# Moving the output projection's parts ahead of the value products in TensorE's slot

## The reference

```python
o = concatenate([diff_attn(...), dsa_attn(...)], axis=-1)
m = o @ w_out
x = x + ga1 * rms_norm(m, g_post_mix)
```

## Time and profile before

| | |
|---|---|
| time, median of 3 runs | 1704.54 us (1704.43 to 1708.21) |
| the profiled execution's own time | 1709.16 us |
| its span, first to last instruction | 1707.4 us |
| its mean granted TensorE clock | 0.964 of full speed |
| PE / PEld / DVE / ACT / POOL busy | 91% / 76% / 44% / 32% / 23% of the span |

### The profile page before, as it was taken

How to read it: one execution, slowest core, us unless ns; L and a number is a source line. 1 busy time by engine, 2 the same in 40 slices (tenths; PEclk the granted TensorE clock), 3 DMA queues, 4 the chain that set the end, 5 groups by cost and what they waited for, 6 DMA issues and landing times.

```text
span 1707.4 us, 23915 instructions
## 1 busy us (share of the span) xinstructions
PE 1561.9 (91%) x8999; PEld 1297.4 (76%) x9019; DVE 749.9 (44%) x1751; ACT 547.8 (32%) x1134; POOL 393.7 (23%) x335
## 2 busy tenths in 40 slices
PE   5699999995788989998769999999999999999996
PEld 2486899994344555555439999999999999999995
DVE  0603799996856665565460312213022130311305
ACT  1735322212355565565362111122111211212112
POOL 0511111110011111011146221323223132231325
PEclk9999999996699999999779999999999999999998
DMA  8310357615333444242251201102111011110006
GB/s 273 99 44 26 107 170 225 188 65 184 102 102 114 129 116 142 88 127 57 69 175 57 67 26 49 49 25 59 40 49 49 25 49 49 49 43 30 0 1 123
DMA packets 148567, 146.94 MB, mean 86 GB/s; under 512 B 12125, under 2 KB 129182, under 8 KB 148490
## 3 DMA queue, kind: packets, MB, share of 16 engines
q1 hardware_dynamic: 147258, 141.46, 28.0%
q0 software_dynamic: 1232, 4.46, 1.4%
HBM read 126.60 MB, written 19.29 MB: 85 GB/s over the span
## 4 chain that ended last, share of the span: by engine, by line
PE 84%; DVE 5%; issue 3%; ACT 3%; DMA 2%; POOL 2%; SPq 1%; POOLq 0%; DVEq 0%; ACTq 0%
PE S L1951 31%; PE PJ L1707 15%; PE T L1966 11%; PE PJ L1870 7%; PE PJ L1966 5%; PE S L1809 4%; PE T L1787 2%; PE PJ L1911 2%; PE PJ L1914 2%; DMA ada_more<-in_w_ada 1%; DVE sc L1511 1%; PE S L1656 1%; PE S L1726 1%; DVE scrap L1338 1%; ACT aT L1120 1%
## 5 line engine op out<-in xcount | busy, mean ns | idle before, releaser
L1951 PE MATMUL S<-h2h,gh 128*128 128x352 f32 (+1 forms) x1056 | 346.6, 328 | 2.0 <-DVE top L1594 2.0
L1951 PE MATMUL S<-h2h,gl 128*128 128x352 f32 (+1 forms) x1056 | 345.9, 328 | 0.0
L1951 PE MATMUL S<-h2l,gh 128*128 128x352 f32 (+1 forms) x1056 | 345.6, 327 | 0.0
L1619 DVE TENSOR_TENSOR hv<-sg,S 128x352 f32<-128x352 f32 (+1 forms) x66 | 35.1, 532 | 496.5 <-ACT sg L1250 496.5
L1951 PEld LDWEIGHTS S<-h2h,gh 128*128 128x128 f32 x1056 | 198.8, 188 | 2.6 <-issue 2.2
L1951 PEld LDWEIGHTS S<-h2l,gh 128*128 128x128 f32 x1056 | 199.5, 189 | 0.4
L1951 PEld LDWEIGHTS S<-h2h,gl 128*128 128x128 f32 x1056 | 198.5, 188 | 0.0
L1338 DVE TENSOR_SCALAR_CACHE_REDUCE scrap<-work,cand 128x384 uint8<-128x384 f32 (+6 forms) x217 | 180.1, 884 | 1.1
L1707 PE MATMUL PJ<-hTh,wh 128*128 128x352 f32 (+3 forms) x504 | 168.9, 335 | 0.0
L1707 PE MATMUL PJ<-hTh,wl 128*128 128x352 f32 (+3 forms) x504 | 166.0, 329 | 0.0
L1707 PE MATMUL PJ<-hTl,wh 128*128 128x352 f32 (+3 forms) x504 | 166.0, 329 | 0.0
(11 more groups left out here) (207 smaller groups left out, 2406.3 us busy)
## 6 DMA issues: line engine op xcount, KB each, us to landing
graw<-in_w_gu SPq DMA_DIRECT2D x44, 512.0 KB, 4.9
ada<-in_w_ada SPq DMA_DIRECT2D x20, 1024.0 KB, 7.6
draw<-in_w_down SPq DMA_DIRECT2D x22, 512.0 KB, 3.3
wraw<-in_w_in SPq DMA_DIRECT2D x20, 512.0 KB, 5.5
q_scratch<-qst SPq DMA_DIRECT2D x8, 544.0 KB, 2.9
xin<-in_x_p SPq DMA_DIRECT2D x8, 512.0 KB, 3.5
ada_more<-in_w_ada SPq DMA_DIRECT2D x4, 1024.0 KB, 12.3
xt<-in_x_p SPq DMA_DIRECT2D x8, 512.0 KB, 4.8
```

The lines of the kernel that those rows point to most:

```text
L1951: last = pe.matmul(S[u % 2][:, 512 * part:512 * part + n], wp[:, slot, k, 128 * part:128 * part + 128], hp[:, k, c0:c0 + n], start=(k == 0 ...
```

## The change

In every slot that has one, the part of the output projection is issued before the value products and after the transposes; nothing else moves, and no instruction is added or removed. `out_projection` keeps its own waits (the weights, `m_out`, `rank_read`, the freed banks of the head outputs, `o_read`), and the products keep theirs. In slots without a part the order stays as it was.

```diff
@@ -1888,6 +1888,8 @@
                     pe.wait_ge(o_ready, diff_count(s))
                     bank = t_wait_free(pe, ("o", s))
                     pe.transpose(bank[:, 0:r], ob[0:r, s % 2, :], ident[0:r, 0:r]).then_inc(filled(("o", s)), 1)
+                if out_part(slot):
+                    out_projection(*out_part(slot))
                 if 2 <= slot < NSTEPS + 2:
 
                     s = slot - 2
@@ -1914,8 +1916,6 @@
                             last = pe.matmul(PJ[0][0:r, 0:128], aT[0:w, 0, j, 0:r],
                                              vsb[0:w, vt_, 128 * i:128 * i + 128], **edge)
                     last.then_inc(pv_done, 1)
-                if out_part(slot):
-                    out_projection(*out_part(slot))
                 for q in range(2):
                     t = tie_stage(slot, 2 + q)
                     if t and 512 * q < nkeys(t):
```

## The result

| | before | after |
|---|---|---|
| median of 5 runs each, us | 1706.32 (1704.43 to 1708.21) | 1714.17 (1713.48 to 1716.15) |
| the profiled execution's own time, us | 1709.16 | 1713.73 |
| its span, us | 1707.4 | 1712.0 |
| mean granted TensorE clock | 0.964 | 0.965 |

The medians differ by 7.9 us. The ratio is 1.0044 with an interval of 1.0031 to 1.0056, that is 5.3 to 9.6 us slower. The forecast was 3.0 us slower, 1707.5 us, with no measurable change as the likeliest case and a range up to 1711 us, so the range was missed on the slow side. The forecast started from the first three runs of before (1704.54 us); with five runs their median is 1.8 us higher, which explains that much of the distance and not more.

What follows compares the result with a forecast made beforehand. The prediction took TensorE, 84% of the chain that ended last, as the bound. A 5.9 us loss less gains of 1.7 and 1.2 us made +3.0 us on 1704.54 us, so 1707.5 us, range 1703.5 to 1711 us.

Steps and rivals of the forecast that it cites:

- no measurable change: Whole kernel: a difference within 5.1 us (0.3%), which a measurement cannot tell from no change; chance 0.77.
- head chain: Differential head's output: VectorE reads and squares products, GpSimd makes RMS factor, VectorE scales, TensorE transposes; covered by the 3.44 us part.
- the chain's price: From the products' modelled end to the next slot's head transpose: 2.01 us; waits in tiles 1, 2, 3, 8, 5.9 us lost.
- The waits of L1890: Head transpose waits for VectorE's `ob` in slots 4 to 6 of tiles 1, 2, 8, barely 3: 6.5 us become 11 to 12.5 us.
- The first rival: Handover from products to VectorE costs more and larger tiles pay too: 1710.4 us at 0.25 us, 1713.4 us at 0.5 us; chance 0.15.
- the gain of slot 6: The part covers the wait ahead of the products, about 1.2 us in the large tiles' slots 6, of 1.7 us gained.
- The net is 5.9 - 1.7 - 1.2 = +3.0 us: Whole kernel: head transpose loss, less the covered wait ahead of the products, less ScalarE's earlier start in slot 7.
- no stall: `out_projection`'s strictest wait, `m_out` in slot 5: at least 1.5 us lies between in tile 1, the copy takes 0.6 us.
- Other waits of the moved step: `out_projection`'s own waits, now ahead of the products: `m_out`, `o_read` and bank waits all met in time.
- 0.1 to 0.2 us behind it: Sign in the profile after: the part starts this long behind the head transpose in 32 slots.
- The gain of L1827 in slots 7: ScalarE starts its backlog earlier behind the last part, so TensorE waits less for probability copies: 1.2 us gained, ends 0 and 3.9 us.
- one more fall: TensorE's clock falls again after new idle times in tiles 1, 2 and 8: about 3.2 us, 1710.7 us; chance 0.05.

Runs made afterwards that it cites:

- run 1: Against the kernel before, only the parts of slots 3 to 5 moved ahead of the products; slot 6 kept the old order: ratio 1.0051, +8.7 us.
- run 2: Against the kernel before, only the part of slot 6 moved ahead of the products: ratio 0.9991, -1.5 us.
- run 3: Against the kernel before, parts moved only in tiles 4 to 7: ratio 0.9987, -2.2 us.
- run 4: Against the kernel before, parts moved only in tiles 1, 2, 3 and 8: ratio 1.0056, +9.6 us.
- experiment 5: Against the changed kernel, head transpose put behind the part, ahead of the products: 1698.45 us against 1708.05 us before, ratio 0.9944.
- run 7: Changed kernel, but VectorE scales the head by a factor it already has, not waiting for GpSimd's RMS factor: ratio 0.9983 to the kernel before, -2.9 us.
- run 13: Changed kernel, but five of a first part's waits issued at the end of the slot before, behind its products: 1712.90 us against 1708.50 us before.
- run 9: Changed kernel, but the five last waits of each first part issued four times over: 1730.47 us against 1708.79 us for the kernel before.
- run 11: Against the kernel before, head transpose put last, behind products and part: 1731.28 us, ratio 1.0129.
- run 10: Against the kernel before, head transpose put between the products and the part: 1705.82 against 1708.79 us, ratio 0.9979.
- run 8: The changed kernel again, unaltered: 1715.65 us against 1708.05 us for the kernel before, ratio 1.0043.
- run 14: The changed kernel once more, unaltered: 1714.96 us against 1708.50 us for the kernel before, ratio 1.004.
- run 6: Changed kernel, but a first part's semaphore waits issued ahead of the head transpose: ratio 1.0056 to the kernel before, +9.6 us.

## Why the prediction was right and wrong

**Right: what bounds these slots, and what the part covered.** The head chain was hidden under the part and no longer is. Runs 1 to 5 and 7 show it: the loss is in slots 3 to 5 of the short tiles, goes from the time when the chain is shortened, and turns into a gain when the part covers the chain again.

**Right: the chain's price and where it is paid.** The waits of L1890 were to become 11 to 12.5 us and are 11.2 us, 4.7 us more than before where the sum had 5.9 us. Slot by slot they are 1.29 us in (1, 4) for 1.2 forecast, 0.94 for 1.0 in (1, 6), 0.41 for 0.57 in (2, 4), 0.58 for 0.67 in (8, 4); in tile 3, where 0.3 us was forecast, none is new. The first rival, a dearer handover, is out: it is 0.04 us with 128 rows too, and no such wait appears in slots 4 and 5 of tiles 5 to 7.

**Right: the gain of slot 6.** The gap ahead of L1911 in slots (5, 6) and (7, 6) is gone: the products follow the part at once, as in slot (7, 6) after, where the part's 786.14 + 3.60 us is followed at 789.67. L1827 in (1, 7) waits 0.59 us for 0.7 forecast. Run 2 puts the slot at -1.5 us.

```profile
786.14 3.60 PE L1870 MATMUL PJ<-wout,oT 128*128 128x512 f32 x8
789.67 1.53 PE L1913 MATMUL PJ<-aT,vsb 128*64 128x128 f32 x24
```

**Wrong: the sum.** The step that failed is "The net is 5.9 - 1.7 - 1.2 = +3.0 us", and in it "no stall" for the part's own waits, put at nothing. The loss was 6.5 to 7.9 us by the medians of three sets of runs, because three costs are missing from the sum. As read from the traces they are 2.3, 1.3 and 1.5 us. With the chain's 1.2 us less this gives 3.0 + 2.3 + 1.3 + 1.5 - 1.2 = 6.9 us, an estimate, for the 7.1 to 7.9 us that the traces show behind the first moved part.

- *The part's own waits, under "Other waits of the moved step".* I asked only whether each was met ("no stall") and took met waits as free. Before, they stood behind the products, with 0.6 to 1.9 us of TensorE's work queued. After, they stand behind one transpose, often a late one. The sign "0.1 to 0.2 us behind it" in 32 slots came true in 20 (0.11 to 0.21 us): the other 12, all of them first parts, start 0.28 to 0.35 us behind. Run 13 puts the cost at 2.3 us in these slots. The four first parts in slots 5 of tiles 4 to 7 pay nothing; there the head transpose is not late, as in slot (4, 5) after:

```profile
598.34 0.28 PE L1890 MATMUL T<-ident,ob 128*128 128x128 f32 x1
598.45 3.60 PE L1870 MATMUL PJ<-wout,oT 128*128 128x512 f32 x8
```

Tile 3 and tiles 4 to 7 came out 1.6 us worse together than foreseen. Six of the twelve slots stand there, and run 13 got 1.3 us back in them. Run 9 shows the cost itself at 0.05 to 0.07 us per wait in the same twelve slots.
- *Where a stall goes.* The gain of L1827 in slots 7 was counted as final. VectorE, now later against TensorE, took it back: the first transpose of slot (2, 1) waits 1.12 us for 0.60 us before, and (3, 1) 0.79 for 0.45 us. Together with the slots around them this is the +0.52 and +0.74 us of the table. Runs 1 and 2 show whose cost this is: with slot 6 alone moved the two rows are +0.53 and +0.74 us, with slots 3 to 5 alone both are 0.00 us. So it is the give-back of slot 6's own gain, and not a cost of the head chain. The timeline of slot (2, 1) shows what stretched, first before, then after:

```profile
479.90 2.36 POOL L875 TENSOR_TENSOR msb<-msb,xt 128x1024 f32<-128x1024 f32 x1 [1.40 <-DVE msb L1444]
...
481.18 1.22 DVE L1528 TENSOR_SCALAR sc<-sc,rinv 128x256 f32<-128x256 f32 x1
...
482.46 0.44 PE L1787 MATMUL T<-ident,sc 128*128 128x128 f32 x2 [0.60 <-DVE sc L1528]
```

```profile
481.59 2.35 POOL L875 TENSOR_TENSOR msb<-msb,xt 128x1024 f32<-128x1024 f32 x1 [1.84 <-DVE msb L1444]
...
482.37 1.72 DVE L1528 TENSOR_SCALAR sc<-sc,rinv 128x256 f32<-128x256 f32 x1
...
484.14 0.44 PE L1787 MATMUL T<-ident,sc 128*128 128x128 f32 x2 [1.12 <-DVE sc L1528]
```

- *The clock.* I gave one more fall a chance of 0.05 and sought it in the tiles of the new waits. It fell right behind those of tile 1, near 485 us in slots (2, 1) and (2, 2), to its lower level (granted clock 0.50 from 488 to 491 us). The row of the table there is 1.48 us longer; the four products of L1809 took 1.65 us for 0.92 us. Every trace with the changed order in slots 3 to 5 of tile 1 shows a fall between 469 and 500 us, run 7 among them, which was not slower than before. So do runs 2 and 11, where these slots are not moved, and run 2 was not slower either; before, run 3, run 10 and both runs of the order of experiment 5 show none. So this is an added cost of about 1.5 us and not the main cause of the loss. What sets it off is not shown: run 2 has none of the new waits of the head transpose and the same +1.48 us, but its slot (2, 1) begins with a longer wait, 1.13 us for 0.60 us; run 1 has the new waits and not this one. The Trainium skill (TensorE: Matmul & The Clock Gate, Why this matters for your kernels) says that idle gaps of TensorE between bursts bring the low clock back. The trace of the kernel after agrees: the clock fell behind slots in which TensorE idled more than before. Run 2 does not bear it out: from 465 to 485 us its TensorE was busy for 15.99 us, as before, and the clock fell all the same.

```profile
482.44 0.44 PE L1787 MATMUL T<-ident,sc 128*128 128x128 f32 x2 [1.13 <-DVE sc L1528]
```

The row above is slot (2, 1) of run 2. How often the kernel before loses 3 us in slot (8, 3) can't be told from one profile: the traces of the changed kernel in runs 8 and 14 have no such fall there, nor has run 3, whose tile 8 is in the order of before.

**What carried the wrong probability.** Rival 1 had the right outcome with a wrong mechanism. That the missing terms have the same sign may be no accident: I had listed what each instruction waits for and not what is issued, or goes by, while it waits.

## What to carry to other kernels

A dense block whose result no engine needs soon can cover a long chain. Put it ahead of the instruction that waits for the chain, not ahead of the one that starts it; here the same move with the head transpose behind the part gave -10 us instead of +8 us. When a step moves, count its semaphore waits as work of the queue that it moves into: they were free where TensorE had work queued, and cost time where it had just run dry. Before an instruction moves later, look at who waits for its result in an engine that works in order (run 11).

## What the runs showed of the hardware

- A semaphore wait that has long been met took 0.05 to 0.07 us of TensorE's queue: 15 more of them put the next product 0.7 to 1.0 us later in twelve slots, with one transpose of 0.27 to 0.48 us ahead (run 9). In slots (6, 5) and (7, 5), whose head transpose was not late, the same 15 cost nothing. A first part's seven waits or fewer, issued while TensorE idled for VectorE, were not absorbed by its wait (run 6).
- VectorE's scaling of 128 x 256 took 1.22 and 1.72 us instead of 0.34 to 0.35 us where GpSimd's 128 x 1024 addition ran beside it, and in both traces it ended 0.14 to 0.15 us after that addition (482.40 against 482.26; 484.09 against 483.94).
- The handover from TensorE's modelled end to VectorE's read was 0.04 us for 128-row products (slot (2, 3) after) and for 64-row products (slot (8, 3) before and after).
